# A fourth pair by seven products in the down projection, with the extra banks kept and laid by ScalarE

## The reference, cut to what matters

```python
u = rms_norm(h, g_pre_mlp[l])
f = jnp.square(jax.nn.relu(u @ w_up[l])) @ w_down[l]    # 2048 -> 8192 -> 2048
h = h + rms_norm(f, g_post_mlp[l])
```

## Time and profile before

| | |
|---|---|
| median of 3 runs | 2030.66 us |
| the profiled execution | 2031.48 us, span 2029.7 us |
| TensorE busy | 2017.8 us, 99% |
| VectorE busy | 1489.5 us, 73% |
| ScalarE busy | 985.2 us, 49% |
| DMA | mean 192 GB/s |
| w_down1 | 1591.60 to 1674.56 us, two steps of 41.48 us |

### The profile page before, as it was taken

How to read it: one execution, slowest core, us unless ns; L and a number is a source line. 1 busy time by engine, 2 the same in 40 slices (tenths; PEclk the granted TensorE clock), 3 DMA queues, 4 the chain that set the end, 5 groups by cost and what they waited for, 6 DMA issues and landing times.

```text
span 2029.7 us, 28875 instructions
## 1 busy us (share of the span) xinstructions
PE 2017.8 (99%) x10509; PEld 1719.2 (85%) x10509; DVE 1489.5 (73%) x2016; ACT 985.2 (49%) x1275; POOL 83.0 (4%) x91
## 2 busy tenths in 40 slices
PE   9999999999999999999999999999999999999998
PEld 7888898888888888999888888888888888888886
DVE  6766766566756655578999856587877887788887
ACT  6645444565544544433444644554553453354343
POOL 0000102001002000002000000000000000000001
PEclk9999999999999999999999999999999999999999
DMA  9688655655667665555666566655576466467554
GB/s 346 198 202 185 177 157 174 187 175 173 185 198 245 185 196 179 175 177 160 189 198 199 177 219 185 192 166 174 185 236 188 158 206 217 155 207 227 187 198 134
DMA packets 265475, 389.32 MB, mean 192 GB/s; under 512 B 12504, under 2 KB 147032, under 8 KB 264571
## 3 DMA queue, kind: packets, MB, share of 16 engines
q1 hardware_dynamic: 262587, 377.19, 60.9%
q0 software_dynamic: 2624, 10.54, 1.9%
q10 hardware_dynamic: 144, 0.01, 0.0%
HBM read 385.02 MB, written 2.54 MB: 191 GB/s over the span
## 4 chain that ended last, share of the span: by engine, by line
PE 98%; SPq 1%; DMA 1%; DVE 0%; ACT 0%; issue 0%; DVEq 0%
PE acc L701 18%; PE acc L678 17%; PE acc L680 17%; PE acc L679 17%; PE acc L699 10%; PE acc L692 2%; PE acc L691 2%; PE acc L693 2%; PE acc L697 1%; PE aux L730 1%; PE aux L732 1%; PE aux L731 1%; PE acc L730 1%; PE acc L731 1%; PE acc L732 1%; PE aux L1619 1%
## 5 line engine op out<-in xcount | busy, mean ns | idle before, releaser
L532 DVE TENSOR_TENSOR low_rows<-stage_rows,high_rows 128x1024 fp32r<-128x1024 f32 x480 | 575.2, 1210 | 295.6 <-ACT high_rows L518 286.9
L518 ACT ACTIVATE high_rows<-stage_rows 128x1024 fp32r<-128x1024 f32 x480 | 495.5, 1040 | 542.2 <-PE acc L680 480.8
L518 ACT ACTIVATE w_high<-stage 128x1024 fp32r<-128x1024 f32 (+1 forms) x264 | 276.1, 1047 | 405.1 <-PE acc L701 298.0
L532 DVE TENSOR_TENSOR w_low<-stage,w_high 128x1024 fp32r<-128x1024 f32 (+1 forms) x264 | 319.8, 1221 | 176.1 <-ACT w_high L518 171.5
L701 PE MATMUL acc<-u,w_high 128*128 128x512 f32 x900 | 247.9, 394 | 0.0
L701 PE MATMUL acc<-hT,w_high 128*128 128x512 f32 x645 | 177.5, 394 | 0.0
L701 PEld LDWEIGHTS acc<-u,w_high 128*128 128x128 f32 x900 | 152.9, 189 | 19.0
L699 PEld LDWEIGHTS acc<-u,w_low 128*128 128x128 f32 x960 | 146.8, 188 | 20.5
L699 PE MATMUL acc<-u,w_low 128*128 128x256 f32 x960 | 152.5, 281 | 0.0
L678 PE MATMUL acc<-high_rows,hT 128*128 128x512 f32 x384 | 151.8, 395 | 0.0
L680 PE MATMUL acc<-high_rows,hT 128*128 128x512 f32 x384 | 149.6, 390 | 0.0
(11 more groups left out here) (451 smaller groups left out, 3601.4 us busy)
## 6 DMA issues: line engine op xcount, KB each, us to landing
stage_rows<-in_w_in SPq DMA_DIRECT2D x160, 512.0 KB, 3.8
stage<-in_w_in SPq DMA_DIRECT2D x136, 512.0 KB, 3.6
stage_rows<-in_w_down SPq DMA_DIRECT2D x128, 512.0 KB, 4.4
stage<-in_w_up SPq DMA_DIRECT2D x120, 512.0 KB, 4.5
stage_rows<-in_w_o SPq DMA_DIRECT2D x64, 512.0 KB, 4.1
stage_rows<-in_w_pool_out SPq DMA_DIRECT2D x16, 512.0 KB, 3.9
stage_rows<-in_w_conv_out SPq DMA_DIRECT2D x16, 512.0 KB, 4.4
stage_rows<-in_w_mem_kv SPq DMA_DIRECT2D x14, 512.0 KB, 11.2
```

What stands on the lines that cost most here:

```text
L518: act.activation(high[:, pr, k_from:kt, 0:p.cols], src[:, slot, k_from:kt, 0:p.cols], ACT.Copy).then_inc(high_done, 1)
L532: dve.tensor_tensor(low[:, pr, k_from:kt, 0:p.cols], src[:, slot, k_from:kt, 0:p.cols], high[:, pr, k_from:kt, 0:p.cols].bitcast(F32), ALU ...
```

## The change

A fourth pair of each step goes by seven products, pair 3, and the order becomes: pair 0 directly (two slabs), 2 and 3 by seven, 1 and 4 directly, 5 and 6 by seven, 7 directly; 24 places. The first LEFT is at idx 2, the last INNER at idx 21. For a sevenfold pair right behind another the sums of its weights are made two or three slabs earlier in VectorE's order. A fourth feature sum is made in each w_up.

VectorE's bank sums are gone. ScalarE copies the banks out in every step, two at idx 21 and two at idx 22 (`keep_z`), and from q = 1 on it copies what was kept back into the banks before they are used again (`lay_z`): for step 0 at slabs 4 and 5 of w_up, for step 1 at idx 0 (banks 0, 1) and idx 1 (banks 2, 3) of that step. TensorE then adds to the banks without starting them anew, and its first LEFT waits for the four lays.

```diff
-SEVENS = (2, 4, 6)
-SEVEN_ORDER = ((0, 1), (2,), (3,), (4,), (5,), (6,), (7,))
+SEVENS = (2, 3, 5, 6)
+SEVEN_ORDER = ((0,), (2,), (3,), (1, 4), (5,), (6,), (7,))
...
-                        SUMS_BEFORE.update({n + 1: (OUTER, n), n + 2: (INNER, n)})
+                        second = job.kinds[idx - 1] == INNER
+                        SUMS_BEFORE.setdefault(n - 2 if second else n + 1, []).append((OUTER, n))
+                        SUMS_BEFORE.setdefault(n - 1 if second else n + 2, []).append((INNER, n))
...
-                if e == 0 and step:
-                    if step <= 2:
-                        pe.wait_ge(s("z_copied"), 4 * step)
-                    else:
-                        pe.wait_ge(s("z_summed"), 4 * (step - 2))
+                if e == 0 and step == 1:
+                    pe.wait_ge(s("z_copied"), 4)
+                elif e == 0 and step:
+                    pe.wait_ge(s("z_laid"), 4 * (step - 1))
...
-                pe.matmul(bk, x_high, high, start=own and e == 0, stop=False)
...
+                laid = own and step >= 2
+                pe.matmul(bk, x_high, high, start=own and e == 0 and not laid, stop=False, skip_group_check=laid)
...
+            def lay_z(q, step, banks):
+
+                act.wait_ge(s("z_copied"), 4 * (2 * q + step))
+                for b in banks:
+                    act.activation(aux[:, b, :], z_rows[step][b][:], ACT.Copy).then_inc(s("z_laid"), 1)
+
+            def keep_z(q):
...
                 def beside(n):
                     step, idx = n // job.S, n % job.S
-                    for b in {inner: (0, 1), inner + 2: (2, 3)}.get(idx, ()):
+                    if q and step and idx < 2:
+                        lay_z(q, step, (2 * idx, 2 * idx + 1))
+                    for b in {inner: (0, 1), inner + 1: (2, 3)}.get(idx, ()):
                         act.wait_ge(used, PAIRS + job.slab0 + step * job.S + inner + 1)
                         act.activation(z_rows[step][b][:], aux[:, b, :], ACT.Copy).then_inc(s("z_copied"), 1)
                 return beside
 
+            def lay_first(q):
+
+                def beside(n):
+                    if n in (4, 5):
+                        lay_z(q, 0, (2 * n - 8, 2 * n - 7))
+                return beside
+
             for q in range(4):
-                rounding(f"w_up{q}", beside=beside_up0 if q == 0 else None)
-                rounding(f"w_down{q}", beside=copy_z(q) if q == 0 else None)
+                rounding(f"w_up{q}", beside=lay_first(q) if q else beside_up0)
+                rounding(f"w_down{q}", beside=keep_z(q))
...
-            def sum_z(q):
...
-                splitting(f"w_down{q}", down_body(q, f"w_down{q}"), beside=sum_z(q) if q else None, at_once=True)
+                splitting(f"w_down{q}", down_body(q, f"w_down{q}"), at_once=True)
```

More of the change, by code:

```diff
@@ L280, in build @@
         y_rows = at("y_rows", Z + 16, [P, 2, D])
-        f_sums = at("f_sums", Z + 32, [P, len(SEVENS), 2, 4, P], F32R)
+        sums_at = [(Z + 32 + 4 * e, Z + 34 + 4 * e) for e in range(3)] + [(74.25, 82.75)]
+        f_sums = [[at(f"f_sums{e}{half}", kb, [P, 4, P], F32R) for half, kb in enumerate(places)] for e, places in enumerate(sums_at)]
         f_raw = at("f_raw", 72.25, [P, 4, P])
@@ L524, in subtract_low @@
             if isinstance(n, int) and n in SUMS_BEFORE:
-                weight_sums(dve, *SUMS_BEFORE[n])
+                for kind, left in SUMS_BEFORE[n]:
+                    weight_sums(dve, kind, left)
             dve.wait_ge(high_done, n + 1)
@@ L552, in sevens_before @@
         def sevens_before(n):
-            return sum(1 for at, (kind, _) in SUMS_BEFORE.items() if kind == INNER and at < n)
+            return sum(1 for sums in SUMS_BEFORE.values() for kind, left in sums if kind == INNER and left < n)
         def stream(eng, split, name, body=None, chain=None, links=0, beside=None, lead=None, hold=0, at_once=False):
@@ L722, in seven_products @@
             x4 = [p.rows[:, k0 + 1, half, P:2 * P] for half in range(2)]
-            sums = [[f_sums[:, e, half, r, :] for half in range(2)] for r in range(4)]
+            sums = [[f_sums[e][half][:, r, :] for half in range(2)] for r in range(4)]
             products = {LEFT: [(0, x1, aux[:, 0, :], True), (1, x2, acc[:, 2 * one, :], False)],
@@ L729, in seven_products @@
                 high, low = high_rows[:, pr, k, :], low_rows[:, pr, k, :]
-                pe.matmul(bk, x_high, high, start=own and e == 0, stop=False)
-                pe.matmul(bk, x_high, low, start=False, stop=False)
-                mm = pe.matmul(bk, x_low, high, start=False, stop=own and e == len(SEVENS) - 1)
+                laid = own and step >= 2
+                pe.matmul(bk, x_high, high, start=own and e == 0 and not laid, stop=False, skip_group_check=laid)
+                pe.matmul(bk, x_high, low, start=False, stop=False, skip_group_check=laid)
+                mm = pe.matmul(bk, x_low, high, start=False, stop=own and e == len(SEVENS) - 1, skip_group_check=laid)
             mm.then_inc(used, 1)
@@ L1439, in beside_last @@
                 if r is not None:
-                    act.wait_ge(s("z_summed"), 21)
+                    act.wait_ge(s("z_spread"), 1)
                     down_squares(r)
@@ L1453, in down_squares @@
                         act.activation(out_rs[:, t:t + 1], out_rs[:, t:t + 1], ACT.Sqrt).then_inc(s("chain_root"), 1)
-            def copy_z(q):
+            def lay_z(q, step, banks):
[3 more added lines that the diff above has]
+            def keep_z(q):
                 job = jobs[f"w_down{q}"]
@@ L2578, in feature_sums @@
                 link(dve.tensor_tensor(f_raw[:, 3, :], f[:, 2, :], f_raw[:, 2, :], ALU.subtract))
-                link(dve.tensor_copy(f_sums[:, e, 0], f_raw[:]))
-                dve.tensor_tensor(f_sums[:, e, 1], f_raw[:], f_sums[:, e, 0].bitcast(F32), ALU.subtract).then_inc(s("f_sums_ready"), 1)
+                link(dve.tensor_copy(f_sums[e][0][:], f_raw[:]))
+                dve.tensor_tensor(f_sums[e][1][:], f_raw[:], f_sums[e][0][:].bitcast(F32), ALU.subtract).then_inc(s("f_sums_ready"), 1)
             def down_body(q, name, first=0):
@@ L2616, in z_spread @@
                     link(dve.tensor_tensor(y22, y22, z5[:], ALU.subtract))
-            def sum_z(q):
[L2619 to L2633, removed]
             def spread(name, step, n):
                 if n in SPREAD_AT[name]:
-                    dve.wait_ge(s("z_summed"), 16 if step else 20)
+                    dve.wait_ge(s("z_copied"), 24 if step else 28)
                     z_spread(step, SPREAD_AT[name].index(n))
@@ L2642, in beside_last @@
                 if n == SPREAD_AT["w_down_last"][-1]:
-                    dve.sem_inc(s("z_summed"), 1)
+                    dve.sem_inc(s("z_spread"), 1)
             def last_down():
```

## The result

The changed kernel took 2044.65 us (median of 6 runs, 2043.36 to 2044.97), the kernel before 2030.75 in the same comparison: +13.9 us, ratio 1.0066 with a 95% interval from 1.0053 to 1.0079. It is slower, by more than the noise. Forecast were 2043.2 and +12.5.

The account below looks back on a forecast made before the run. TensorE, busy 99% of the span, was taken as the bound, with VectorE near its limit. -4.76 + 11.2 + 1.07 + 5.04 = +12.5 us on the median 2030.66 gave 2043.2 us, range 2037.5 to 2048.0.

Parts of the forecast that it names:

- The gain: TensorE in seven w_down steps: one more sevenfold pair saves 3 matmuls per step, 21 in all, -4.76 us.
- The entrances: From w_up into w_down, four times: TensorE pauses 1.53 us at slab 4, 1.09 at slab 5, with restarts 2.80; +11.2 us.
- Step 1 of w_down0: Start of that step: VectorE's queue makes slab 5 late by 0.98 us plus 0.09 restart, +1.07 us.
- The lays: Step 1 of w_down1 and w_down2: TensorE waits before LEFT for ScalarE's copies, 2.52 us each, +5.04 us.
- The DRAIN rule: VectorE's burst: next operation waits for an empty pipe; at 1.22 us each, burst 0.6 us longer, sum 15.4.
- slabs 14 to 21: Around sevenfold pairs 5 and 6, behind four direct slabs: no pause, by at least 0.7 us.
- the keeps, the first lays: Copies out at idx 21 and 22, and lays for step 0 in w_up: no time cost.
- the fourth feature sum: In each w_up: 2.18 us more of VectorE per q, zero cost in time.
- the loads: Slab 7 lands 8 us before the sum for OUTER of pair 3 needs it: zero cost.
- rival 4: More pauses than counted, from late landings or at pairs 5 and 6; 1 us in seven steps gives 2050; 11%.
- Rival 3: Lays don't pause, but VectorE's burst pauses TensorE in every step: +9.6 us, 2040.3; 5%.
- the burst fits: VectorE's queue entering w_down causes no pause: 2025.9 us if the lays fit too (7%), 2030.9 if they pause (7%).

Follow-up runs that it names:

- e3: Kernel before (three sevenfold pairs, old order) with ScalarE's keeps and lays in place of VectorE's bank sums: 2030.89 us against 2030.94, ratio 0.9999.
- e1: Changed kernel with the lays for step 1 of w_down1 and w_down2 two places earlier: 2041.46 us, ratio 1.0048 to the kernel before.
- e2: Changed kernel with the weight sums of each sevenfold pair behind a direct one made one slab earlier in VectorE's order: 2040.84 us, ratio 1.0048.
- e6: Changed kernel with ScalarE copying banks 2 and 3 twice in step 1 of w_down1 and w_down2: 2049.37 us, ratio 1.0094.
- e10: Kernel before (three sevenfold pairs) with the first of them at idx 2 and the change's keeps and lays: 2039.54 us against 2031.4, ratio 1.0043.
- e7: Changed kernel with the early lays of e1 and the weight sums of pairs 3 and 6 made by GpSimd: 2056.09 us, ratio 1.0126.
- e9: Changed kernel with e1's lays, sevenfold and direct pairs alternating, weight sums spread, OUTER's behind a direct pair before slab n - 1: 2032.34 us, ratio 1.0004.
- e4: Changed kernel with the early lays of e1 and first pairs' sums two slabs earlier, OUTER before n - 1, INNER before n: 2036.54 us, ratio 1.0026.

## Why the prediction was right, by its own steps

- **The gain, -4.76 us**: right. 21 matmuls of 0.2267 us; TensorE ran at that distance wherever it ran at full clock, but for the dozen matmuls behind a pause.
- **The entrances, 2.80 us each**: 2.47 + 0.22 = 2.69. The pauses of 1.53 and 1.09 were 1.43 and 1.04, the restart 0.11 in place of 0.09. VectorE's row by row times were those of before, to 0.01; the release of TensorE behind a split came 1.28 us after its start, not 1.36, which the one row of the first stage had given.
- **Step 1 of w_down0, 1.07**: 1.03 + 0.11 (0.18 over the dozen matmuls behind it).
- **The lays, 2.52 each**: 2.42 + some 0.1. A copy into a bank takes 582 ns. That is the end of the bounds that the Trainium skill (ScalarE: Activation LUTs, "Step-by-step: what each stage is for") pointed to when it calls PSUM the faster place to write to. The row of 627 ns that gave the other end is a sigmoid, not a copy; of the copies from SBUF to SBUF the half rounding is one of this size, and takes 625 in the changed kernel, so the bound was right.
- **The DRAIN rule** of the Trainium skill (VectorE: DVE Perf Modes, "The DRAIN you can't avoid"): rows of 1.22 us start 1.14 apart throughout the burst, as before, so the trace doesn't show the rule as the prediction put it. The same section adds that a next operation starts earlier unless it is held, and so it is here. The 15.4 us by the rule is as near to the measured 13.9 as the forecast's 12.5, for a wrong reason.
- **Nothing at slabs 14 to 21, nothing for the keeps, the first lays, the fourth feature sum, the loads**: right; the changed kernel has eleven pauses in w_down, all in the places named, w_up1 keeps its 89.70 us, and e3 shows the banks' part at nothing.
- **The range and rival 4**: what was missing from the sum is the clock, 1.57 us in the profiled execution. The prediction had the pauses and not what may follow one. From w_down0's start on the two profiles differ by 14.1; less the clock that is 12.5, as forecast.
- **Rival 3** is what e1 builds: 2040.3 forecast, 2041.46 measured. The rivals that began with "the burst fits" fell with the first timeline.

What stays open: what decides whether the clock halves behind a pause. In four profiles with lay pauses (the changed kernel, e2, e6, e10) it did so behind one of two each time, the one in w_down2. Lays are not needed for it: in e7 it followed the two waits on VectorE at the entrance of w_down3, in e9 one of 2.12 us in the first stage. And length doesn't sort the cases: it stayed full behind 2.93 us in e7, behind 2.06 in the first stage of the changed kernel, and behind every pause of 1.43. Whether the spread of the runs, 1.6 us in the changed kernel, comes from it was not shown: the mean clock of the runs speaks for it in e10 and e6, but not in the changed kernel, whose longest run, 2044.97, has 0.999.

## What to carry to other kernels

Look not only at an engine's busy share but at its queue, item by item, where work is bunched: here 38.2 of 40.8 us on average hid a burst of 8.0 us with 5.5 us to be ready in. When a helper's result gates the bound engine, look at what its queue puts in front of it; two copies of 0.58 us cost 2.4 because a rounding that waited on TensorE itself stood ahead of them. And where the helper is near its limit, moving its work earlier only pays as far as it idles there and nothing else waits behind it; e4 gave back in bank releases, at the start of step 1, what it won there in sums.

## What the runs showed of the hardware

- With GpSimd adding fp32 tiles in SBUF beside it (e7), VectorE's split took 2.62 us in place of 1.22, a half split 2.87 in place of 0.68 and a cast 1.40 in place of 0.43, while its reduction out of PSUM kept 1.21. I had expected idle GpSimd time to be free.
- After a pause of 2.4 us TensorE ran at half of its clock for about 3.5 us in one of two cases in each of three profiles, 1.6 us lost in the changed kernel, with the engine at full clock before the pause; after 3.6 us too it was one of two. In e9 it did so after 2.1 us.
- A restart behind a wait on VectorE costs TensorE 0.11 us more at once (the second matmul 0.33 to 0.34 behind the first, nine times alike) and 0.13 to 0.18 over a dozen matmuls; behind the lay pause at full clock it was 0.07 and 0.10.
- ScalarE writes a 128x512 tile from SBUF to PSUM in 582 ns, as fast as it reads one from there (584), and 43 ns faster than its copy with rounding of a tile of this size from SBUF to SBUF (625).
